# Down projection of a decoder layer: plain K tiles against a seven-product block scheme in four chunks

## What is computed

```
proj = x @ w_in + b_in                                  # q, k, v and a GLU pair
mix  = concat(window attention, conformer conv) @ w_out + b_out
x    = layer_norm(ALPHA * x + mix, ln1_g, ln1_b)
h    = causal_dwconv3(x @ ffn_w_up)                     # 2 * D_FF columns
f    = (silu(h_gate) * h_up) @ ffn_w_down               # the stage that is changed
y    = layer_norm(ALPHA * x + f, ln2_g, ln2_b)
```

## Time and profile before

| | us |
|---|---|
| median of 3 runs (2148.28 to 2150.33) | 2148.54 |
| the profiled execution | 2148.49 |
| its span | 2146.6 |
| TensorE matmuls busy in it | 2067.5 (96%) |
| VectorE, ScalarE, POOL busy | 1415.4, 909.5, 429.3 |
| share of the chain that ended last: TensorE; up projection L866; down projection L929 | 86%; 41%; 22% |

### The profile page before, as it was taken

How to read it: one execution, slowest core, us unless ns; L and a number is a source line. 1 busy time by engine, 2 the same in 40 slices (tenths; PEclk the granted TensorE clock), 3 DMA queues, 4 the chain that set the end, 5 groups by cost and what they waited for, 6 DMA issues and landing times.

```text
span 2146.6 us, 41639 instructions
## 1 busy us (share of the span) xinstructions
PE 2067.5 (96%) x16125; PEld 2038.2 (95%) x16125; DVE 1415.4 (66%) x1916; ACT 909.5 (42%) x1264; POOL 429.3 (20%) x544
## 2 busy tenths in 40 slices
PE   8999999799995999999999999999999999999995
PEld 8999999699985999999999999999999999999994
DVE  3788888677599777777777777777864222334224
ACT  4344454433466454545455555455444111222223
POOL 0113122020631221222121222121121000004222
PEclk9999999799998999999999999999999999999998
DMA  6322222023656767676767676766658222332222
GB/s 222 105 79 74 73 73 79 29 69 100 205 157 207 196 177 194 177 192 172 197 175 193 176 192 170 198 178 190 180 185 290 91 84 88 120 109 85 90 74 83
DMA packets 93499, 307.41 MB, mean 143 GB/s; under 512 B 11940, under 2 KB 12708, under 8 KB 93408
## 3 DMA queue, kind: packets, MB, share of 16 engines
q1 hardware_dynamic: 74832, 242.70, 34.3%
q0 software_dynamic: 17424, 61.44, 15.0%
q10 hardware_dynamic: 1152, 1.96, 0.2%
HBM read 282.10 MB, written 23.97 MB: 143 GB/s over the span
## 4 chain that ended last, share of the span: by engine, by line
PE 86%; DVE 7%; issue 3%; ACT 2%; DMA 1%; POOL 0%; SPq 0%; ACTq 0%; DVEq 0%; POOLq 0%
PE acc L866 41%; PE acc L929 22%; PE acc L583 15%; PE acc L779 3%; PE acc L592 1%; PE acc L679 1%; PE acc L668 1%; PE acc L659 1%; DVE resid L2043 0%; DVE w_lo L1694 0%; ACT w_hi L974 0%; DVE tb L1662 0%; DVE w_lo L1776 0%; PE acc L655 0%; ACT xn L1138 0%
## 5 line engine op out<-in xcount | busy, mean ns | idle before, releaser
L866 PE MATMUL acc<-comb,w_hi 128*128 128x274 f32 x4816 | 925.1, 291 | 23.0 <-DVE comb L1826 18.0
L866 PEld LDWEIGHTS acc<-comb,w_hi 128*128 128x128 f32 x4816 | 762.5, 189 | 25.0 <-issue 12.3
L866 PE MATMUL acc<-comb,w_lo 128*128 128x274 f32 x2408 | 696.5, 289 | 0.0
L929 PE MATMUL acc<-acts,w_hi 128*128 128x272 f32 x2752 | 460.2, 289 | 5.1 <-DVE resid L1987 2.2
L866 PEld LDWEIGHTS acc<-comb,w_lo 128*128 128x128 f32 x2408 | 459.9, 191 | 0.0
L929 PEld LDWEIGHTS acc<-acts,w_hi 128*128 128x128 f32 x2752 | 390.6, 189 | 6.1 <-issue 3.5
L929 PE MATMUL acc<-acts,w_lo 128*128 128x272 f32 x1376 | 284.9, 289 | 0.0
L1218 ACT ACTIVATE w_hi<-sum 128x1024 fp32r<-128x1024 f32 x172 | 182.3, 1060 | 225.1 <-PE acc L866 120.5
L1776 DVE TENSOR_TENSOR w_lo<-sum,w_hi 128x1024 fp32r<-128x1024 f32 x172 | 210.6, 1224 | 91.2 <-ACT w_hi L1218 88.1
L1776 DVE TENSOR_TENSOR w_lo<-raw_a,w_hi 128x1024 fp32r<-128x1024 f32 x127 | 155.2, 1222 | 97.6 <-ACT w_hi L1218 97.5
L929 PEld LDWEIGHTS acc<-acts,w_lo 128*128 128x128 f32 x1376 | 216.3, 188 | 0.0
(11 more groups left out here) (250 smaller groups left out, 2801.6 us busy)
## 6 DMA issues: line engine op xcount, KB each, us to landing
raw_a<-w_up SPq DMA_DIRECT2D x127, 512.0 KB, 6.3
stage<-w_stream SPq DMA_DIRECT2D x90, 512.0 KB, 3.5
sum<-w_up POOLq DMA_DIRECT2D x89, 512.0 KB, 7.3
sum<-w_up SPq DMA_DIRECT2D x88, 512.0 KB, 3.5
sum<-w_down SPq DMA_DIRECT2D x45, 448.0 KB, 3.2
sum<-w_down SPq DMA_DIRECT2D x24, 512.0 KB, 3.5
act_spill<-prod_f SPq DMA_DIRECT2D x43, 272.0 KB, 6.2
act_raw<-act_spill POOLq DMA_DIRECT2D x43, 272.0 KB, 4.0
```

The costliest lines, as they stand in the source:

```text
L866: mm = pe.matmul(bank(BANK_OF[j]), wt[:, k * P:(k + 1) * P], prod_comb(j, k, b), start=start and q == 0, stop=stop and q == 2, skip_group_ ...
L929: mm = pe.matmul(acc[:, a, h, 0:D_TOK // 2], wt[:, w * P:(w + 1) * P], x[:, h * (D_TOK // 2):(h + 1) * (D_TOK // 2)], start=start and q == ...
```

## The change

The down projection is made like the up projection, by seven products in place of eight, but in chunks of K.

- The first three K tiles (`F_TILES`) stay plain: 16 groups, one per output row, of 3 x 6 matmuls (`first_tile`). ScalarE copies each row from PSUM to `resid` with the factor 1/ALPHA. While these run, the items of chunk 0 are made.
- The other 40 tiles are four chunks of five pairs (`CHUNKS`, `PAIRS`); pair p joins tile t and tile t + 5. For each chunk there are eight blocks b, i = b % 8; a block makes output rows i and i + 8. A product is 15 matmuls of 272 columns into one bank, seven products per block, in the order `ORD`, some of them accumulating on what stands in the bank.
- After each product VectorE adds the bank, with a sign and 1/ALPHA, to a quadrant of `resid` (two rows by two token halves), so `resid` holds (ALPHA x + f) / ALPHA. The norm's epsilon is divided by ALPHA squared. The residual x is added by eight adding DMAs of POOL's queue, after the blocks of chunk 0 (`add_x1`).
- The data items of a pair are four sums and seven high and low parts of 272 columns: `t_one` to `t_four` and `item_low` on VectorE, `raw_top` and `sum_item_top` on ScalarE. They are made during the chunk before. Eight slots per item kind hold a chunk of five and three of the next; the last two pairs have to wait until the old chunk's last block has used its items (`item_free`), and come in its last block and the next one's first (`pair_work`).
- Weights come in quarters of 640 columns: five loads (a11, a12, a22, and the first terms of S1 and S3) on SP, two adding loads (S1, S3) on POOL, S2 and S4 on VectorE.
- The norm's preparation moves to chunk 3: two rows per block are shifted by VectorE, squared by ScalarE, summed by POOL.

The core of the diff:

```diff
-K_CUT = ((0, 22), (22, FT))
-OUTER = 4
+F_TILES = 3
+PAIRS = 5
+CHUNKS = 4
+N_FIRST = KT
+DOWN0 = N_UP + N_FIRST
+N_BLOCKS = CHUNKS * 8
+LAST8 = N_BLOCKS - 8
+ORD = (0, 4, 1, 2, 3, 6, 5)
+D_BANKS = ((0, 1, 2), (4, 5, 3))
...
-            def down_row(n, w, a, t, start, stop):
...
+            def bank_free(b, s):
+                done = N_PROD * b
...
+                if s == 0 and b >= 2:
+                    pe.wait_ge(down_added, done - N_PROD)
+                if s in (2, 4, 6):
+                    pe.wait_ge(down_added, done + s - 1)
+                if s == 5:
+                    pe.wait_ge(down_added, done + 4)
+
+            def down_product(b, s):
+                n, j, c = DOWN0 + N_PROD * b + s, ORD[s], b // 8
+                a = D_BANKS[b % 2][(0, 2, 0, 1, 0, 1, 0)[s]]
+                pe.wait_ge(up_lo, n + 1)
+                if b % 8 == 0:
+                    pe.wait_ge(item_lo[j], PAIRS * (c + 1))
+                bank_free(b, s)
+                for e in range(PAIRS):
+                    p = PAIRS * c + e
+                    for q, (wt, lo) in enumerate(((whi(n), 0), (whi(n), 1), (wlo(n), 0))):
+                        mm = pe.matmul(bank(a, 0, HD), wt[:, e * P:(e + 1) * P], item(j, p, lo),
...
+                mm.then_inc(up_used, 1)
...
+                if b == N_BLOCKS - 1 and s == N_PROD - 1:
+                    ln_stats_begin(2)(4)
...
+            ln_stat_tile(2, 0)
             ln_stats_end(2)
...
+            def pair_work(b, s):
+                c, i = b // 8, b % 8
+                k = 7 * (i - 1) + s
+                late, now = PAIRS * (c + 1) + 3, PAIRS * c + 3
+                if c + 1 < CHUNKS and 0 <= k < 33:
+                    early_pair(PAIRS * (c + 1) + k // 11, k % 11)
+                if c + 1 < CHUNKS and i == 7:
...
+            def add_product(b, s):
+                n, i = N_PROD * b + s, b % 8
...
+                dve.wait_ge(up_used, DOWN0 + n + 1)
...
+                dve.scalar_tensor_tensor(out=r, in0=bank(D_BANKS[b % 2][(0, 2, 0, 1, 0, 1, 0)[s]], 0, HD), scalar=sign / ALPHA, in1=r,
+                                         op0=ALU.mult, op1=ALU.add).then_inc(down_added, 1)
...
+            for b in range(N_BLOCKS):
+                for s in range(N_PROD):
+                    if s:
+                        add_product(b, s - 1)
+                    elif b:
+                        add_product(b - 1, N_PROD - 1)
+                    pair_work(b, s)
+                    low_after(b, s)
+                    if s == 1:
+                        make_d_s4(b)
+                    if s == 5 and b + 1 < N_BLOCKS:
+                        make_d_s2(b + 1)
+                    if b == LAST8 and s == 3:
+                        shift_row(8)
...
+                    if LAST8 <= b < N_BLOCKS - 1 and s in (4, 5):
+                        shift_row(b - LAST8 + 1 + 8 * (s - 4))
...
+            def add_x1(i):
+                pool.wait_ge(down_added, N_PROD * (i + 1))
...
+                pool.dma_start(resid[:, i:KT:8, D0:], dram["x1_spill"][:, i::8, :], accum_op=ALU.add).then_inc(x1_added, 16)
...
+                if b > LAST8:
+                    for q in range(2):
+                        sums(2 * (b - LAST8 - 1) + q)
```

More of the change, by code:

```diff
@@ L921, in _ @@
                 up_block(f, N_PROD * f)
-            def down_row(n, w, a, t, start, stop):
-                hi, lo = act_part(t, 0), act_part(t, 1)
-                for q, (wt, x) in enumerate(((whi(n), hi), (whi(n), lo), (wlo(n), hi))):
-                    for h in range(2):
-                        mm = pe.matmul(acc[:, a, h, 0:D_TOK // 2], wt[:, w * P:(w + 1) * P], x[:, h * (D_TOK // 2):(h + 1) * (D_TOK // 2)],
-                                       start=start and q == 0, stop=stop and q == 2)
-                return mm
@@ L960, in _ @@
-                mm.then_inc(up_used, 1)
-                if (c, m, i) == (1, OUTER, 0):
-                    pe.wait_ge(acc_added, KT + 1)
-                    stat(0, 2, resid[:, 0, :], D_CUT).then_inc(shift_mm, 1)
+                pe.wait_ge(f_lo_made, F_TILES)
+                first_free(d)
+                for t in range(F_TILES):
+                    for q, (wt, x) in enumerate(((whi(n), f_hi), (whi(n), f_lo), (wlo(n), f_hi))):
+                        for h in range(2):
+                            mm = pe.matmul(acc[:, d % 4, h, 0:HD], wt[:, t * P:(t + 1) * P], x[:, t, h * HD:(h + 1) * HD],
+                                           start=t == 0 and q == 0, stop=t == F_TILES - 1 and q == 2)
@@ L1420, in _ @@
[L1420 to L1429 removed]
+                    silu(f)
+                if d >= 2:
+                    first_row_out(d - 2)
@@ L1430, in _ @@
+            for b in range(N_BLOCKS):
+                for s in range(N_PROD):
+                    top_after(b, s)
+                    pair_tops(b, s)
+                    if b == LAST8 and s == 1:
+                        shift_out(2, 3, ln_shift2)
+                    if b > LAST8 and s in (0, 2):
+                        square(2 * (b - LAST8 - 1) + s // 2)
+            square(KT - 2)
+            square(KT - 1)
             mean_out(2, 0, 3)
@@ L1631, in variance @@
                 mean = AL(a - 1, which) if which else halves(ln_mu[:, t])
-                st.did(dve.tensor_tensor(halves(ln_sqs[which][:, 1, t]), mean, halves(ln_mu[:, t]), ALU.mult))
+                st.did(dve.tensor_tensor(halves(ln_sqs[which][:, 1, t]), mean, halves(ln_mus[which][:, t]), ALU.mult))
                 st.wait()
@@ new lines, in pair_work @@
+            def pair_work(b, s):
+                c, i = b // 8, b % 8
+                k = 7 * (i - 1) + s
+                late, now = PAIRS * (c + 1) + 3, PAIRS * c + 3
+                if c + 1 < CHUNKS and 0 <= k < 33:
+                    early_pair(PAIRS * (c + 1) + k // 11, k % 11)
+                if c + 1 < CHUNKS and i == 7:
+                    for p in (late, late + 1):
+                        if s in (2, 3):
+                            item_low((0, 4)[s - 2], p)
+                        if s == 4:
+                            t_one(p)
+                        if s == 5:
+                            t_three(p)
+                    for p in (late, late + 1):
+                        if s == 4:
+                            t_two(p)
+                        if s == 5:
+                            t_four(p)
+                        if s == 6:
+                            item_low(1, p)
+                            item_low(2, p)
+                if c > 0 and i == 0:
+                    for p in (now, now + 1):
+                        if s == 0:
+                            item_low(3, p)
+                        if s == 1:
+                            item_low(6, p)
+                            item_low(5, p)
```

638 lines of the change are left out of this document (419 added, 219 removed).

## The result

| | before | changed |
|---|---|---|
| median of 4 runs, us | 2149.21 (2148.28 to 2150.33) | 2114.33 (2112.82 to 2117.78) |
| span of the profiled execution | 2146.6 | 2113.0 |
| mean granted clock of TensorE | 0.985 | 0.981 |

The ratio is 0.984, interval 0.9823 to 0.9857: 35 us faster, where 52 were forecast. The direction and the range held; the time is 18 us above the forecast of 2096.

The account below looks back on a forecast made before the run. TensorE's instruction count was taken to bound the down projection. From 2148.5 us, matmuls -60.6, old idle time -5.1, statistics -1.1, borders +7.5, last chunk +4 and begin +3 sum to -52.3: 2096 us, range 2083 to 2122.

Parts of the forecast that it names:

- Matmuls, -60.6: Down projection: 3648 matmuls, 480 fewer, at 0.1263 us each, saving 60.6 us.
- Statistics at the end: Norm statistics at the stage's end: three sets between last product and mean, 0.7 more there; -1.1 us in all.
- VectorE's pace: Blocks with items: VectorE needs 11.7 of 13.26 us in the mean, so TensorE sets the pace; cost 0.
- Rival 1: VectorE sets the pace: waiting instructions cost full duration, 13.4 us a block, chunks end 5 us later; 2110 us, chance 0.12.
- Chunk borders, +7.5: Three chunk changes: VectorE's debt grows by 4.0 us, TensorE bears about 1.4, leaving 2.5 each; bounds 0 and 15.
- Last chunk, +4: Row shifts on VectorE beside POOL's sums stretch both; 0.5 us lost in each of 7 blocks; bounds 0 and 19.
- The bound of 19: Upper bound for the last chunk: VectorE's and POOL's work does not overlap at all, 2.6 us a block.
- the rule by mean load: Last chunk under the skill's exclusive lock: only additions of products overlap, 13.4 us a block, +1 in place of +4.
- Begin of the stage, +3: Down projection's start: fourth first tile 1 us late, perhaps 2, fifth row waiting for stored states about 1; bounds 0 and 8.
- DMA, 0: Weight and pair loads: 9.9 us of 13.26 a block, share 0.75, covered by TensorE; cost 0.
- Rival 2: The a12 weight quarter lands 10.6 us after issue, so each of 32 blocks waits 3 us; 2192 us, chance 0.06.
- The clock, rival 3: Borders and last-chunk blocks each cost a low-clock piece, 10 x 1.4 = 14 us; 2110 us, chance 0.05.

Follow-up runs that it names:

- e8_all: Changed kernel with the last chunk's 28 sums made by VectorE and ScalarE's activation high parts put behind the up projection's last high parts: 2086.11 us.
- e5_no_shift: Changed kernel without VectorE's 16 row shifts in the last chunk, POOL's sums left in their bursts: 2105.96 us.
- e7_sums_noshift: Changed kernel with the 28 sums on VectorE, ScalarE's activation high parts later, and the 16 row shifts left out: 2084.2 us.
- e2_no_sums: Changed kernel without POOL's 28 sums of rows and squares in the last chunk (the final norm's statistics are then wrong): 2090.67 us.
- e3_memsets: Changed kernel with each of POOL's 28 sums replaced by three memsets that read nothing (statistics wrong): 2090.78 us.
- e1_late_tops: Changed kernel with ScalarE's three activation high parts put behind the last two weight high parts of the up projection: 2110.34 us.
- e4_spread: Changed kernel with POOL's 28 sums spread over products 0, 2, 3 and 6 of a block, adding DMAs between them: 2101.91 us.

## Why the prediction was right and wrong

*Matmuls, -60.6: right.* There are 3648 matmuls. In e8_all the 3360 of the products start from 1623.9 on, and the statistics behind them at 2055.46: 431.6 us. Less 2.4 of waits and three sets of statistics in the stream (0.71, 0.91 and 0.72 from start to start) that is 426.9, or 0.1271 each, where the prediction had 0.1263. The difference is 2.5 us in all. The 288 matmuls of the plain tiles took 0.6 us less than forecast (35.8 us from 1591.69 to 1627.50 in the changed kernel), so that the term was 2 us too good.

*Statistics at the end: right.* The last product ends at 2084.27 in the changed kernel, and the last set of statistics starts at 2086.86:

```profile
2084.11 1.08 PE L952 MATMUL acc<-resid,ones 128*128 128x272 f32 x4
...
2086.86 1.08 PE L952 MATMUL acc<-sq,ones 128*128 128x272 f32 x4
```

The mean is copied at 2087.06, 2.8 us after the product, the three sets forecast. The time from the last product to the end of the span is 28.8 us, 28.1 before: the 0.7 forecast.

*VectorE's pace: right.* 272 columns start 0.35 apart (2002.01 to 2002.36 above) and 640 columns 0.73. In chunks 1 and 2 it is busy for 98 and 97 of 108 us, 12 in a block, and TensorE loses 1.2 a chunk. Rival 1, VectorE pacing every block, fell: chunk 0 has no gap. Its price was not sound either: 13.4 against 13.26 is 1.1 us in eight blocks, not 5.

*Chunk borders, +7.5: too high.* They cost 2.0: 1.01 at 1736.21 and 1.02 at 1843.73, both behind low parts, as forecast in kind. VectorE's debt was sized right. It can be read from the time between the end of a product's last matmul and its addition: 0.21 us at product 3 of block 7, then 0.81, 2.15, 2.76, in the next block 2.66, and 2.75 at its product 1 (from 1738.34, the end of the second row, to 1741.09):

```profile
1736.21 0.52 PE L1088 MATMUL acc<-comb,w_hi 128*128 128x272 f32 x2 [1.01 <-DVE w_lo L2192]
...
1738.06 0.28 PE L1088 MATMUL acc<-comb,w_lo 128*128 128x272 f32 x1
...
1741.09 0.43 DVE L2317 SCALAR_TENSOR_TENSOR resid<-acc,resid 128x272 f32<-128x272 f32 x1
```

With the time that TensorE itself lost before that product (1.2) the debt grew by 3.7, where I had 4.0, and in the steps forecast. The step that failed is what TensorE can bear: an addition 2.76 late did not stop it, where I allowed 1.4, which asked only what one product's turn allows. At the third border the addition of product 0 is only 1.69 late and there is no pause: a set of statistics (L745, at 1949.03) lies in TensorE's stream and takes 0.7 us. A further pause of 0.46 at 1963.08 is no border's: it stands behind two row shifts and is gone in e5_no_shift and e7_sums_noshift, which have none.

*Last chunk, +4: the step that failed.* It cost 24 (23.7 by e2_no_sums, and the 0.46 of the shifts). The prediction had POOL and VectorE share, with VectorE getting "a little over half done", and took a mean over the block. Three things were wrong with it. The two take turns: VectorE stands until POOL's instruction is over, 1.14 us a sum, and spread evenly that alone is 11.2. The mean was not enough, since the order puts the four sums in a row on the turn with most to do; the burst makes 23.7 of the 11.2. And the clock fell after long pauses, to 0.87 and 0.93 in two windows of 25 us, which is some 5 of the 12.5 that the burst adds. By the traces the sum is: 17.7 us of waits from 1974 to 2084, 5.0 of clock, and some 2 because a wait shows only from the end of a matmul's 0.29 us, 0.16 after the next one was due (12 times, an estimate), against 25.1 measured. The bound of 19 fell because it laid the two engines' work end to end over a whole block and priced neither burst nor clock.

The Trainium skill, "SBUF — State Buffer", section "Who interferes with whom", says just this, an exclusive lock where the loser blocks, for instructions with two SBUF inputs; the trace agrees, with low part, S2 and shift held at 3.52, 1.96 and 1.86, and the addition out of PSUM at 0.42. I had put sharing above it on the strength of the earlier trace rows, where 1.88 in place of 0.72 can be read either way. The trace of the kernel before could have told, had I set the ends side by side:

```profile
1940.72 2.02 POOL L2136 TENSOR_TENSOR ln_sum<-ln_sum,resid 128x544 f32<-128x544 f32 x1
...
1942.70 1.84 POOL L2140 TENSOR_TENSOR ln_sq<-ln_sq,sq 128x544 f32<-128x544 f32 x1
```

The first ends at 1942.74, the shift of the earlier trace rows at 1943.33, 0.59 later; the second ends at 1944.54, 1.21 after the shift. Both stretched, but by turns. But the rule by mean load gave +1, further off still: it says who waits, and the order of the instructions says how much.

*Begin of the stage, +3: the size near, the mechanism wrong.* The plain tiles start at 1591.7, 5.1 later than before. Of that 3.4 is the pause, and the rest fits the clock: 0.94 over 27 us is 3.2 us at the lower level, half of which is lost (an estimate). Neither the fourth tile nor the states made a pause. What did was the queue behind ScalarE's first activation top, issued early for data that was still 6.77 us away. The prediction followed moved instructions on VectorE and not what stood behind a wait on ScalarE.

*DMA, 0: right* for the weights, though the load is not what I worked out: a share of 0.96 in chunk 0, where the residual is added and items are read ahead, 0.80 and 0.74 after, against 0.75. Quarters take 4.5 us to land and the adding loads 6.8, by the page; no wait of TensorE's in the stage leads to one; the activations read back before it are another matter (the begin). Rival 2, the late quarter, fell.

*The clock, rival 3:* it did not act at bank changes or at the borders, where it is 1.00 all through, but it took its part at the begin and in two windows of the last chunk. A granted clock under 1.00 inside the stage was named as a sign of being wrong, and rightly.

**The sum again:** 2096.2, with +24.1 for +4, +2.0 for +7.5, +5.1 for +3 and 1.9 for the matmuls' distance, is 2114.8; measured 2114.33. The forecast was 18 us short, a third of the gain that it promised, because one term was six times too small. That the time lies in the range is luck in part: the last chunk was outside its own bound, and the borders, 5.5 too high, made up for some of it. With borders as forecast the time would have been 2120, just inside the upper end.

Three things stay open: whether the two pauses left at the borders go when the late pairs' items are cut down, whether reading alone, at the same length, makes POOL's instruction block, and which pauses bring the clock down, since one of 2.6 us at 2019.03 left it at 1.00 in its window. None was tried.

## What to carry to other kernels

- Beside a VectorE that is 80% busy with SBUF inputs, POOL was no free helper for elementwise sums. Count each of its instructions that has inputs in SBUF as blocking VectorE for its own time, and ask which turn it falls on: what stands before it in POOL's order decides that. Here 28 sums made on VectorE were 25 us cheaper than on POOL.
- An instruction that waits for a DMA holds all that is behind it on its engine. Put early work for the next stage behind the last urgent work of this one.

## What the runs showed of the hardware

- A 640-column subtraction of VectorE took 3.52 us between two POOL sums of 1.77 and 1.76, and 0.82 alone. Beside three POOL clears in a row an addition of 640 columns kept its 0.82 and a shift of 544 its 0.72 (e3_memsets).
- Where the two met, each ended about its own time after the other: VectorE 0.58 to 0.69 us after POOL, POOL 1.21 and 1.22 after VectorE. An addition with one source in PSUM kept its 0.43 beside a sum.
- Chunk 0 ran with the DMA engines 96% busy at 240 GB/s, and TensorE waited for none of it.
- Of the three windows of the last chunk that hold a pause of 2.6 us, two had a granted clock of 0.87 and 0.93, the third 1.00; in e1_late_tops, with pauses of up to 3.5 us, four windows from 1975 to 2075 had 0.93, 0.93, 0.90 and 0.89; with pauses of at most 1.7 us (e4_spread, e5_no_shift) it stayed at 1.00 there.
